# Hybrid step, even mixer: the gate projection behind v and u, the last tile's recurrence and the gated products between the gate pairs

## What is computed

```
u, v, gate, xr = split(h @ w_in, [512, 1024, 1536])           # h: 640 x 1024, w_in: 1024 x 2048
ya = gelu(u) * (ws_h @ rmsnorm(gelu(v)) + bs)                 # gMLP in chunks of 128 tokens, 4 head groups
for d in (forward, backward):
    xc = dwconv(xr, conv_w[d], conv_b[d])                      # 4 taps
    r, i = sigmoid(xc @ wa[d] + ba[d]), sigmoid(xc @ wi[d] + bi[d])
    log_a = 8 * r * log_sigmoid(lam[d])
    h_t = exp(log_a) * h_(t-1) + sqrt(1 - exp(2 log_a)) * i * xc
yb = (h_forward + h_backward) * gelu(gate)
y  = concat(ya, yb) @ w_out                                    # 640 x 1024
```

## Time and profile before

| | |
|---|---|
| median of 3 runs | 1626.31 us (1625.92 to 1627.29) |
| profiled execution, its own time | 1626.48 us |
| its span in the trace | 1624.7 us |
| mean granted clock of TensorE | 0.965 of 2.4 GHz |
| PE busy | 1502.4 us (92%) |
| DVE, ACT, POOL busy | 657.5, 553.6, 517.4 us |

### The profile page before, as it was taken

The page is one execution under the profiler, slowest core; times in us unless marked ns, Lnnn a source line. Parts: engine busy times, 40 slices in busy tenths (PEclk is TensorE's granted clock), DMA queues, the critical chain, the costliest instruction groups (busy, mean ns, idle before and its releaser), DMA issues.

```text
span 1624.7 us, 20071 instructions
## 1 busy us (share of the span) xinstructions
PE 1502.4 (92%) x8338; PEld 1240.6 (76%) x8338; DVE 657.5 (40%) x1124; ACT 553.6 (34%) x927; POOL 517.4 (32%) x224
## 2 busy tenths in 40 slices
PE   4799879899999999999789789989899999999997
PEld 1787646697898999897567656657699889989985
DVE  3665662732322322232744466623542222223235
ACT  3455732631221232221522266524532213222311
POOL 0521233142243243232314234413343324323430
PEclk8899989899999999999899999999899999999999
DMA  9322435144342222134151100033232122213221
GB/s 337 98 78 104 136 86 172 41 150 143 130 149 94 95 78 78 52 104 143 42 177 62 49 1 1 2 104 130 66 129 73 58 78 80 77 55 101 78 87 69
DMA packets 90498, 153.87 MB, mean 95 GB/s; under 512 B 6356, under 2 KB 44704, under 8 KB 90408
## 3 DMA queue, kind: packets, MB, share of 16 engines
q1 hardware_dynamic: 81712, 143.14, 26.7%
q10 hardware_dynamic: 8696, 9.45, 2.0%
HBM read 149.69 MB, written 2.89 MB: 94 GB/s over the span
## 4 chain that ended last, share of the span: by engine, by line
PE 70%; DVE 8%; ACT 5%; issue 2%; POOL 2%; DMA 1%; ACTq 0%; DVEq 0%
PE PS L1159 20%; PE PS L1160 20%; PE PS L1161 20%; PE PS L1199 2%; PE PS L1397 2%; POOL WL L864 2%; DVE ACC L977 1%; PE PS L1389 1%; DVE X L978 1%; PE PS L1367 1%; PE PS L1350 1%; PE PS L1368 1%; ACT XCB L681 1%; DVE HL L998 1%; DMA RAW<-in_w_qkv 1%
## 5 line engine op out<-in xcount | busy, mean ns | idle before, releaser
L864 POOL TENSOR_TENSOR WL<-RAW,WH 128x1024 fp32r<-128x1024 f32 x172 | 421.3, 2480 | 765.3 <-ACT WH L640 765.3
L1159 PE MATMUL PS<-HH,WH 128*128 128x384 f32 (+1 forms) x1152 | 359.9, 312 | 9.5 <-DVE HL L998 5.3
L1160 PE MATMUL PS<-HL,WH 128*128 128x384 f32 (+1 forms) x1152 | 358.9, 312 | 0.0
L1161 PE MATMUL PS<-HH,WL 128*128 128x384 f32 (+1 forms) x1152 | 358.8, 311 | 0.0
L640 ACT CAST WH<-RAW 128x1024 fp32r<-128x1024 f32 x172 | 170.1, 1046 | 497.5 <-PE PS L1161 337.9
L1159 PE MATMUL PS<-WH,AH 128*128 128x512 f32 x640 | 251.8, 393 | 10.4 <-DVE ACC L1080 10.4
L1160 PE MATMUL PS<-WL,AH 128*128 128x512 f32 x640 | 250.3, 391 | 0.0
L1161 PE MATMUL PS<-WH,AL 128*128 128x512 f32 x640 | 250.2, 391 | 0.0
L1159 PEld LDWEIGHTS PS<-HH,WH 128*128 128x128 f32 x1152 | 221.8, 193 | 14.9 <-issue 8.7
L1160 PEld LDWEIGHTS PS<-HL,WH 128*128 128x128 f32 x1152 | 221.7, 192 | 0.5
L1161 PEld LDWEIGHTS PS<-HH,WL 128*128 128x128 f32 x1152 | 221.5, 192 | 0.0
(11 more groups left out here) (160 smaller groups left out, 1549.7 us busy)
## 6 DMA issues: line engine op xcount, KB each, us to landing
RAW<-in_w_mod SPq DMA_DIRECT2D x42, 1024.0 KB, 5.2
RAW<-in_w_ffn_in SPq DMA_DIRECT2D x32, 1024.0 KB, 5.6
RAW<-in_w_ffn_out SPq DMA_DIRECT2D x32, 1024.0 KB, 4.9
RAW<-in_w_in_even SPq DMA_DIRECT2D x8, 1024.0 KB, 6.8
RAW<-in_w_qkv SPq DMA_DIRECT2D x6, 1024.0 KB, 5.3
EARLY_H<-in_w_mod SPq DMA_DIRECT2D x4, 1024.0 KB, 21.2
RAW<-in_w_out_even SPq DMA_DIRECT2D x4, 1024.0 KB, 5.8
RAW<-in_w_out_odd SPq DMA_DIRECT2D x4, 1024.0 KB, 5.1
```

What stands on the lines that cost most here:

```text
L864: nc.gpsimd.tensor_tensor(ring_view(WL, ld, j), w_view(ld, b), ring_view(WH, ld, j).bitcast(f32), ALU.subtract).then_inc(w_lo, 1)
L1159: MM(out, wh, xh, start=first, stop=False)
L1160: MM(out, wh, xl, start=False, stop=False)
L1161: return MM(out, wl, xh, start=False, stop=last)
```

## The change

The steps of the even mixer get another order, and some results other buffers:
- gate 0-1 no longer follow xr; v comes at once. The new order: xr 0-1, xr 2-3, v0, rg(0,0), v1, rg(0,1), root 0, fill 0, v2, v3, v4, rg(1,0), u0, rg(1,1), root 1, vnorm, fill 1, u1, u2, rg(2,0), fill 2, u3, rg(2,1), root 2, u4, gate 0-1, rg(3,0), rg(3,1), fill 3, gmlp, root 3, ya 0 to 2, modfin, gate 2-3, ya 3, ya 4, wout with its two mods.
- POOL only sums the directions, straight into `GT[j]`; DVE multiplies by the gelu of gate and makes the low parts. The gelu of gate tiles 0 and 1 goes to `GT[3]`, so that of tile 1 waits for the product of tile 0; those of tiles 2 and 3 go to `XC`. The sum of tile 3 goes to `GT[3]` and waits for both products.
- yb's high parts go to `YBH` and its low parts to `YBL` (in `MX`, where xr and gate lay), ya's to `YAH` (the half of ACC where v lay) and `YAL`. wout reads these.
- ACT waits before a tile's sigmoids for the sum (`h_sum`) and no longer for the product (`rg_done`).

```diff
-    apair("gate", 0, ("w_in",), 1024)
-    for d in (0, 1):
-        step("rg", uses_a=2, tile=0, d=d)
-    step("root", tile=0)
-    apair("gate", 2, ("w_in",), 1024 + 256)
-
-    halves = [(1, 0), (1, 1), None, (2, 0), (2, 1), None, (3, 0), (3, 1)]
+    def rg(tile, d):
+        step("rg", uses_a=2, tile=tile, d=d)
+    def root(tile):
+        step("root", tile=tile)
     fill = [(0, 3, 0), (0, 3, 1), (0, 4, 0), (0, 4, 1)]
+    after = {("v", 0): [(rg, 0, 0)], ("v", 1): [(rg, 0, 1), (root, 0), (mod, *fill[0])], ("v", 4): [(rg, 1, 0)],
+             ("u", 0): [(rg, 1, 1), (root, 1)], ("u", 2): [(rg, 2, 0), (mod, *fill[2])], ("u", 3): [(rg, 2, 1), (root, 2)]}
     for what, nb in (("v", 1), ("u", 0)):
         j = bload(("w_in",), nb)
         for t in range(TT):
             bgroup(what, nb, t, j)
-            if what == "u" and t == 2:
+            for act_, *spec in after.get((what, t), []):
+                act_(*spec)
+            if (what, t) == ("u", 0):
                 step("vnorm", uses_m=1)
-            half = halves.pop(0) if halves else None
...
-            if t in (0, 2):
-                mod(*fill.pop(0))
+                mod(*fill[1])
+    ld = load("acols", src=("w_in",), col=1024)
+    ld2 = load("acols", src=("w_in",), col=1024 + 256)
+    apair("gate", 0, ("w_in",), 1024, None, ld)
+    for d in (0, 1):
+        rg(3, d)
+    mod(*fill[3])
     step("gmlp", uses_a=4)
-    step("ya", uses_m=1, t=0)
-    step("ya", uses_m=1, t=1)
+    root(3)
+    for t in range(3):
+        step("ya", uses_m=1, t=t)
     flush()
+    apair("gate", 2, ("w_in",), 1024 + 256, None, ld2)
+    for t in range(3, TT):
+        step("ya", uses_m=1, t=t)
...
+        YBH, YBL = (MXR[:, c:c + 2560].rearrange("p (j n) -> p j n", j=4) for c in (0, 2560))
+        YAH, YAL = ACCR[:, :, 512:1024], MXR[:, 5120:7680].rearrange("p (t n) -> p t n", t=TT)
...
+            return GT[:, 3, :] if tile < 2 else XC[tile - 2]
...
-                            nc.scalar.activation(GT[:, tile, :], a_bank(a), ACT.Gelu_apprx_tanh).then_inc(a_free[a % 2], 1)
+                            if tile == 1:
+                                act.wait_ge(yb_made, 1)
+                            elif tile > 1:
+                                act.wait_ge(xc_used, 8)
+                            nc.scalar.activation(gate_of(tile), a_bank(a), ACT.Gelu_apprx_tanh).then_inc(a_free[a % 2], 1)
...
+                    for tile in (s["tile"], s["tile"] + 1) if s["what"] == "gate" else ():
+                        act.wait_ge(yb_made, tile + 1)
+                        nc.scalar.copy(YBH[:, tile, :], GT[:, tile, :]).then_inc(yb_hi, 1)
...
-                        act.wait_ge(rg_done, j)
+                        act.wait_ge(h_sum, j)
...
                     pool.wait_ge(h_ready, 2 * j + 2)
-                    upto(pool, a_free, GATE_A[j])
-                    nc.gpsimd.tensor_tensor(TH[0], TH[0], TH[1], ALU.add).then_inc(h_sum, 1)
-                    pool.wait_ge(h_sum, j + 1)
-                    nc.gpsimd.tensor_tensor(GT[:, j, :], GT[:, j, :], TH[0], ALU.mult).then_inc(rg_done, 1)
+                    if j == 3:
+                        pool.wait_ge(yb_made, 2)
+                    nc.gpsimd.tensor_tensor(GT[:, j, :], TH[0], TH[1], ALU.add).then_inc(h_sum, 1)
...
+                    if s["what"] == "gate":
+                        pair = (s["tile"], s["tile"] + 1)
+                        for tile in pair:
+                            upto(dve, a_free, s["a"] + tile - pair[0])
+                            dve.wait_ge(h_sum, tile + 1)
+                            V_.tensor_tensor(GT[:, tile, :], GT[:, tile, :], gate_of(tile), ALU.mult).then_inc(yb_made, 1)
+                        for tile in pair:
+                            dve.wait_ge(yb_hi, tile + 1)
+                            V_.tensor_tensor(YBL[:, tile, :], GT[:, tile, :], YBH[:, tile, :].bitcast(f32), ALU.subtract).then_inc(yb_lo, 1)
```

More of the change, by code:

```diff
@@ L217, in schedule @@
             bgroup("wout", nb, t, j, ph=1)
-            if nb == 0 and t + 2 < TT:
-                step("ya", uses_m=1, t=t + 2)
             if nb == 0 and t in (0, 2):
@@ L340, in hybrid_step @@
         MX = alias("MX", [P, 2 * AS * TOK])
+        MXR = alias("MXR", [P, 2 * AS * TOK], f32r)
         AH = sb("AH", [P, AS, TOK], f32r)
         AL = sb("AL", [P, AS, TOK], f32r)
+        ACCR = alias("ACCR", [P, TT, D], f32r)
         ACC = sb("ACC", [P, TT, D])
@@ L431, in hybrid_step @@
         h_ready, h_sum = sem("h_ready"), sem("h_sum")
-        xc_used, ea_ready, t_ready, root_ready, rg_done = (sem("xc_used"), sem("ea_ready"), sem("t_ready"), sem("root_ready"),
-                                                            sem("rg_done"))
+        xc_used, ea_ready, t_ready, root_ready = sem("xc_used"), sem("ea_ready"), sem("t_ready"), sem("root_ready")
+        yb_made, yb_hi, yb_lo, ya_hi = sem("yb_made"), sem("yb_hi"), sem("yb_lo"), sem("ya_hi")
         vs_ready, vn_ready, wst_in = sem("vs_ready"), sem("vn_ready"), sem("wst_in")
-        mix_hi, mix_lo = sem("mix_hi"), sem("mix_lo")
+        mix_hi = sem("mix_hi")
         l1_in = [sem(f"l1_in{i}") for i in range(4)]
@@ L468, in hybrid_step @@
         KT_M = [s["m"] for s in STEPS if s["kind"] == "kT"][-1]
-        GATE_A = [s["a"] + i for s in STEPS if s["kind"] == "A" and s["what"] == "gate" for i in (0, 1)]
         SHEET_M = [s["m"] for s in STEPS if s["kind"] == "sheet"][0]
@@ L477, in hybrid_step, with gate_of @@
         QKV_B = [s["b"] for s in STEPS if s["kind"] == "B" and s["what"] == "qkv"][-1]
+        def gate_of(tile):
+            return GT[:, 3, :] if tile < 2 else XC[tile - 2]
         def step_done(eng, s):
@@ L659, in _ @@
                         else:
-                            act.wait_ge(rg_done, 4)
+                            act.wait_ge(h_sum, 4)
+                            if s["half"] == 0:
+                                with nc.allow_non_contiguous_dma(reason="1024 state values, features on the partitions"):
+                                    act.dma_start(A["new_state"], NS[:, :]).then_inc(stored, 16)
                         g = A["norm_mix_post" if kind == 0 else "norm_ffn_post"][s["layer"]:s["layer"] + 1, 512 * half:512 * half + 512]
@@ L785, in _ @@
                     nc.scalar.activation(SV[:, :, 1:2], SV[:, :, 0:1], ACT.Sqrt, scale=1.0 / 512, bias=EPSC[:, :]).then_inc(vs_ready, 1)
[L786 to L793, removed]
                 elif k == "ya":
@@ L796, in _ @@
                     act.wait_ge(m_ready[u % 2], u // 2 + 1)
-                    nc.scalar.copy(HH[:, 0:4, t * P:t * P + P], m_bank(u).rearrange("p (k n) -> p k n", k=4)).then_inc(mix_hi, 1)
+                    nc.scalar.copy(YAH[:, t, :], m_bank(u)).then_inc(ya_hi, 1)
                 elif k == "kT":
@@ L902, in remainder @@
                 u, g, t = PV_M[i], i % NKV, i // NKV
-                dve.wait_ge(mix_hi, TT + 4 + i + 1)
+                dve.wait_ge(mix_hi, i + 1)
                 cols = slice(t * P, t * P + P)
@@ L1101, in _ @@
                                                 ALU.add, ALU.mult).then_inc(a_free[a % 2], 1)
-                        dve.wait_ge(mix_hi, h + 1)
-                        V_.tensor_tensor(HL[:, 4 + h, :], GT[:, h, :], HH[:, 4 + h, :].bitcast(f32), ALU.subtract).then_inc(mix_lo, 1)
                 elif k == "ya":
                     u, t = s["m"], s["t"]
[L1106 to L1109, removed]
+                    dve.wait_ge(ya_hi, t + 1)
+                    V_.tensor_tensor(YAL[:, t, :], m_bank(u), YAH[:, t, :].bitcast(f32), ALU.subtract).then_inc(m_free[u % 2], 1)
                 elif k == "softmax":
@@ L1269, in _ @@
                         if s["ph"] == 1 and nb == 0:
-                            pe.wait_ge(mix_lo, 4)
                             upto(pe, m_free, YA_M[t])
@@ L1282, in _ @@
                         hs = slice(t * P, t * P + P)
-                        ins = split3(PS[:, 4 + b % 2, :], (HH[:, kt, hs], HL[:, kt, hs]), (WH[:, j % RING, cols], WL[:, j % RING, cols]),
+                        tok = (HH[:, kt, hs], HL[:, kt, hs])
+                        if what == "wout" and s["ph"] == 1 and kt < 4:
+                            tok = (YAH[:, t, P * kt:P * kt + P], YAL[:, t, P * kt:P * kt + P])
+                        elif what == "wout" and s["ph"] == 1:
+                            if nb == 0 and t == 0:
+                                pe.wait_ge(yb_lo, kt - 3)
+                            tok = (YBH[:, kt - 4, hs], YBL[:, kt - 4, hs])
+                        ins = split3(PS[:, 4 + b % 2, :], tok, (WH[:, j % RING, cols], WL[:, j % RING, cols]),
                                      kt == 0, kt == KD - 1)
```

## The result

The changed kernel takes 1650.69 us (median of 4 runs, 1647.14 to 1654.09) against 1626.8 for the kernel before on the same chip (1625.92 to 1628.55): 1.0146 times as long, 95% interval 1.0126 to 1.0165. The forecast was 1647, with 1633 to 1654 as its range. The profiled execution took 1650.28 us with a span of 1648.4, against 1626.48 and 1624.7.

What follows compares the result with a forecast made beforehand. TensorE (PE) was taken as the bound, busy 1502.4 of 1624.7 us. wout starting 24.7 us later, less 4.0 saved behind it and rounding, gave +20.5 on 1626.5: 1647 us, range 1633 to 1654.

Steps and rivals of the forecast that it cites:

- (d): Gates 0 and 1: PE ends them at 201.5; rg(3,0) then waits 2.2 us and rg(3,1) 3.2.
- (e): At mod fill 3: PE waits 3.7 us for its second load, held until gates 2 and 3's low parts are made.
- (f): At the third ya: PE waits 12.6 us for DVE behind root(3), 4.7 of root(3) from POOL; wout starts at 255.
- (a): v and u in front: the wait of 2.7 us at rg(0,1) goes, and v4 starts 0.4 late.
- (b): At u0: 4.2 us of waits for POOL's low parts of u's weights behind root(0); u0 ends at 133.1.
- (c): At mod fill 1: PE waits 17.3 us, until 153.7, for DVE's copy into WST behind root(1); slow clock adds 3.
- The bounds: At the third ya: root(3) ends at 230.6 without POOL's share, or at 235.3 with two low parts, 4.7 us.
- (g): In wout: 4.0 us saved (transposes 1.6, slow clock 1.9, a modfin wait 0.5); the rest of the program unchanged.
- the faster one: Rival: the gates fill the hole at the stretch's end; 17.3 + 3 and 12.6 + 2 go: 1612 us, chance 0.05.
- only (c) binds: Rival: root(3) is done when the gmlp products are through, so 12.6 us go: 1634 us, chance 0.12.
- More contention: Rival: the port holds DVE back at u0 and for all four low parts, landings take 11 us: 1654, chance 0.09.

Runs made afterwards that it cites:

- Experiments 1 and 2: vnorm moved ahead of rg(1,1) and root(1) in the changed kernel, 1640.94 us; vnorm moved behind rg(3,1) and root(3) in the kernel before, 1636.45 us.
- experiment 4: The changed kernel with the casts and low parts of w_out_even's first four blocks issued behind root(3) instead of at mod fill 3: 1648.07 us.
- experiment 5: The changed kernel with the store of the end states issued after layer 1's new_v instead of ahead of the gate norm's loads: 1647.75 us.
- experiment 3: The changed kernel with root(3) placed behind ya 0 to 2 and their modfin in every queue: 1639.17 us.

## Why the prediction was right, and where it was off

The two long waits, their causes and nearly their sizes were forecast, and the time fell in the range. Part of the closeness is luck: (d) and (e) put the start of root(3) 2.4 us too late, (f) made root(3) 2.6 us too short, and so wout came within 0.8 us.

**(a)** held: rg(0,1) does not wait, and v4 waits 0.2 (0.4 forecast).

**(b)** held: four waits of u0 with 3.8 us in all (4.2), its end at 133.3 (133.1).

**(c)** was the step that decided, and it held to the tenth: mod fill 1 starts at 153.76 (153.7) behind 17.30 us. Experiments 1 and 2 show that the bank is the cause.

**(d)** had the mechanism right and one size too large: PE ends gates 0 and 1 at 200.9 (201.5), rg(3,0) waits 0.8 (2.2) and rg(3,1) 2.9 (3.2). These waits have their own price, which the sum left out: with a granted clock of 0.63 from 208 to 211, rg(3,1) takes 3.7 us instead of 2.25. The load of gate 0-1 was ready for ACT at 178.4, not 180.2, so root(2) ended at 201.3, not 203.2: the 7.1 us from the earlier trace rows was the landing of an early stage, 5.5 was the better row.

**(e)** was too large for the most part for the same reason: 1.9 us, not 3.7. The low parts of gates 2 and 3 were done at 209.2, the load landed 5.1 us behind.

**(f)** was right in its mechanism and too small by 1.4: 14.0, not 12.6. The term that was mis-sized is POOL's share, 4.7 for two low parts; ACT had all four casts done at 222.97, since their loads had landed, so POOL had four to give and DVE lost 7.3 (experiment 4). Smaller terms took 1.2 of these 2.6 us back: PE needed only the first of the two remainders, 0.75 us and not 1.5, and reached its wait 1.25 us behind the start of root(3), not 0.8. The bounds were set by two cases, and neither was the worst. wout was put at 255 and came at 254.2.

**(g)** is the step that failed. The 4.0 us were worked out rightly, experiment 5 gives them (4.1), but "the rest of the program is the same" was not true: the change also moves the store of the end states ahead of the gate norm's loads (in lines that the diff above leaves out), and that DMA was not priced at all. It costs two waits for loads, 2.2 us together, and 1.9 of slow clock behind them, by chance just what was to be saved. The profiled execution came 23.8 us over the one before instead of 20.5: these 4.1 less the 0.8 by which wout came early. The store can't be found in the schedule: it hangs on a condition inside ACT's part of `mod`.

The rivals: the faster one is refuted by the 17.3 us, and "only (c) binds" by the 14.0. "More contention" gave 1654 and was half right: POOL did hold DVE back with all four low parts, for 7.3 us, but the awaited loads of the stretch landed in 5.1 to 5.5 us, not in 11.

## What to carry to other kernels

Where banks rotate and each engine has one queue, ask for every use of a bank who frees it and what stands ahead of that instruction in its queue: a copy of 0.7 us behind a chain of 16 is worth 17 on the engine that bounds. A moved block must be read for its conditions too, since a small store can ride on a step that does not name it. And gains of separate edits do not add where one of them only relieved another's wait: the late casts of experiment 4 were worth 6.8 us of the stretch alone, and cost 5.4 where root(3) had been moved as in experiment 3.

## What the runs showed of the hardware that was not expected

A store of 1024 separate values of 4 bytes took 9.1 us to land and held back two 1 MB loads from another engine's queue, issued 5.5 and 8.3 us behind it: they landed 16.2 and 16.0 us after issue, and 5.4 and 7.8 with the store elsewhere. SP's own issue of the second took 3.2 us instead of 0.37.

Scans share the fate of the other DVE operations with two inputs in SBUF: one of 128 columns took 2.44 us beside POOL instead of 0.42, one of 512 took 3.18 instead of 1.28.

In the profiled executions the changed stretch began up to 3 us earlier or later in kernels that are alike up to there; for differences of a few microseconds the length of a stretch told more than the median.
